# Hybrid encoder block: Q and K split where they are projected, both maps' scores of one half of the keys in one block, attention begun between the projection's last groups

## The reference, cut to what matters

```python
hn = rmsnorm(h, norm1_g[l])                     # h is (1, 2048, 1024), float32
proj = hn @ w_in[l]                             # (1, 2048, 2048): q, k, v, u, 512 columns each
q = proj[..., :512].reshape(bsz, s, 4, 2, 64)   # 4 heads, 2 maps, 64 wide
k = proj[..., 512:1024].reshape(bsz, s, 4, 2, 64)
v = proj[..., 1024:1536].reshape(bsz, s, 4, 128)
...
sc = einsum('bqhcd,bkhcd->bhcqk', qi, k) * scale     # two score maps per head, blocks of 128 queries
p = softmax(sc - slope * |qpos - kpos|)
a = p[:, :, 0] - lam * p[:, :, 1]
o = einsum('bhqk,bkhe->bqhe', a, v)
```

## Time and profile before

| what | value |
|---|---|
| device time, median of 3 runs (lowest to highest) | 2686.13 us (2683.91 to 2692.33) |
| profiled execution, span from first to last instruction | 2681.7 us |
| PE busy / DVE / ACT / POOL, share of the span | 96% / 78% / 53% / 12% |
| mean granted clock of PE, share of full speed | 0.981 |
| projection (PE) | 10.1 to 397.3 us |
| attention (PE) | 407.0 to 1006.1 us |
| S5 part, then output projection and MLP | 1009 us to the end |

### The profile page before, as it was taken

One profiled execution on the slowest core, in us unless ns is written; L12 is line 12 of the kernel. 1 busy time (PEld: TensorE's weight loads), 2 busy tenths in 40 slices (PEclk: granted clock), 3 DMA queues, 4 the chain that ended last, 5 costly groups with the idle time before them and its releaser, 6 DMA issues.

```text
span 2681.7 us, 32621 instructions
## 1 busy us (share of the span) xinstructions
PE 2562.9 (96%) x12804; PEld 2155.2 (80%) x12804; DVE 2093.3 (78%) x2074; ACT 1416.5 (53%) x1737; POOL 327.2 (12%) x221
## 2 busy tenths in 40 slices
PE   7998998999999998988989999999999999999998
PEld 5887777999999986766867888888887888888886
DVE  5866638999999976776898877677888886678885
ACT  3276616878787772224444566543334665543334
POOL 6310001101010003320334000000014000000003
PEclk8999998999999999998999999999999999999999
DMA  5356643020204008977565554452234664452221
GB/s 182 111 181 224 221 135 79 25 69 23 72 23 109 24 11 227 267 232 271 186 220 219 220 222 173 173 219 95 94 111 160 247 219 173 173 204 94 94 79 63
DMA packets 162520, 397.17 MB, mean 148 GB/s; under 512 B 29376, under 2 KB 86976, under 8 KB 134592
## 3 DMA queue, kind: packets, MB, share of 16 engines
q1 hardware_dynamic: 145664, 319.06, 35.9%
q10 hardware_dynamic: 16704, 76.03, 7.2%
HBM read 270.79 MB, written 122.16 MB: 147 GB/s over the span
## 4 chain that ended last, share of the span: by engine, by line
PE 44%; DVE 3%; POOL 1%; DMA 1%; issue 1%; ACT 0%; DVEq 0%; SPq 0%; ACTq 0%; POOLq 0%
PE ml_bank L2447 15%; PE ml_bank L2449 15%; PE ml_bank L2448 15%; POOL kp_tabs L2056 1%; DMA kp_low<-hn_s 1%; DVE ml_res L2327 0%; DVE ml_hb L2361 0%; DVE ml_b_split L2258 0%; DVE ml_w_split L2269 0%; DVE ml_res L2347 0%; DVE ml_rinv L2353 0%; PE ml_bank L2455 0%; DMA ml_hb<-h_s 0%; DMA hn_s<-ml_hb 0%; DVE kp_low L2282 0%
## 5 line engine op out<-in xcount | busy, mean ns | idle before, releaser
L2447 PE MATMUL ml_bank<-ml_b_split,ml_w_split 128*128 128x512 f32 x2016 | 788.8, 391 | 10.1 <-issue 9.8
L2448 PE MATMUL ml_bank<-ml_b_split,ml_w_split 128*128 128x512 f32 x2016 | 785.8, 390 | 0.0
L2449 PE MATMUL ml_bank<-ml_b_split,ml_w_split 128*128 128x512 f32 x2016 | 785.7, 390 | 0.0
L2447 PEld LDWEIGHTS ml_bank<-ml_b_split,ml_w_split 128*128 128x128 f32 x2016 | 379.3, 188 | 93.9 <-issue 14.6
L2448 PEld LDWEIGHTS ml_bank<-ml_b_split,ml_w_split 128*128 128x128 f32 x2016 | 379.6, 188 | 79.7 <-issue 1.2
L2449 PEld LDWEIGHTS ml_bank<-ml_b_split,ml_w_split 128*128 128x128 f32 x2016 | 379.4, 188 | 79.2
L2056 POOL TENSOR_TENSOR kp_tabs<-kp_tabs,ml_square 128x512 f32<-128x512 f32 x55 | 144.2, 2622 | 1266.4 <-ACT ml_square L2160 1259.9
L942 ACT ACTIVATE at_e<-at_e,at_neg_top 128x2048 f32<-128x2048 f32 x128 | 256.5, 2004 | 43.8 <-DVE at_neg_top L1027 43.8
L1148 PEld LDWEIGHTS at_pv<-at_v,at_a_t 128*128 128x128 f32 x2048 | 258.3, 192 | 16.4
L2327 DVE TENSOR_TENSOR ml_res<-ml_bank,ml_res 128x2048 f32<-128x2048 f32 x75 | 171.5, 2287 | 118.8 <-PE ml_bank L2449 118.8
L2094 ACT ACTIVATE ml_b_split<-kp_u_t 128x2048 fp32r<-128x2048 f32 x54 | 103.5, 1917 | 298.1 <-PE ml_bank L2449 298.1
(11 more groups left out here) (225 smaller groups left out, 4097.9 us busy)
## 6 DMA issues: line engine op xcount, KB each, us to landing
act_s<-ml_res ACTq DMA_DIRECT2D x32, 1024.0 KB, 4.0
kp_wide<-in_w_stream SPq DMA_DIRECT2D x18, 1024.0 KB, 5.1
kp_bp<-in_w_stream SPq DMA_DIRECT2D x18, 1024.0 KB, 5.5
kp_tabs<-in_w_stream SPq DMA_DIRECT2D x18, 1024.0 KB, 5.9
ml_r<-in_w_stream SPq DMA_DIRECT2D x18, 1024.0 KB, 6.7
tab_s<-kp_tabs ACTq DMA_DIRECT2D x32, 512.0 KB, 2.7
kp_low<-hn_s SPq DMA_DIRECT2D x16, 1024.0 KB, 5.5
kp_u_t<-hn_s SPq DMA_DIRECT2D x16, 1024.0 KB, 4.9
```

The costliest lines, as they stand in the source:

```text
L2447: pe.matmul(out, w_hi[:, w], b_hi[:, b], start=fresh and kt == 0, stop=False, skip_group_check=True)
L2448: pe.matmul(out, w_hi[:, w], b_lo[:, b], start=False, stop=False, skip_group_check=True)
L2449: last = pe.matmul(out, w_lo[:, w], b_hi[:, b], start=False, stop=kt == 3, skip_group_check=True)
```

## The change

What it does, by part:

1. **Split where projected.** For each of the 32 Q and K groups ACT makes the high part from `qku_out` into `v_out` (`keep_high`) and DVE subtracts it in place (`keep_low`); both are stored, to `hi_s` and `lo_s`. The buffers `qku_out` are free for group n+2 when both stores have landed (`stored`).
2. **Loads of the attention.** `load_k` is 8 DMAs of 512 KB per head, straight into `k_hi` and `k_lo`; `load_q` is 4 DMAs of 32 KB straight into `q_hl`, which has 2 buffers; Q of step n+2 is issued when the scores of step n are done. The splitting on ACT, DVE and POOL is gone from the attention. `head.load` is issued at n = 51 instead of 48.
3. **Both maps in one block.** The 8 matmuls of both maps for one half of the keys come together, and a PSUM slot belongs to a map. `combine` is done in two halves.
4. **Attention begins earlier.** Identity, distances, bias and lambda are made during the projection's last groups; K, two Q tiles and V are loaded in them; PE computes the scores of steps 0 and 1 behind groups 60 to 63, DVE their bias and maxima. Projection and attention share one block of instructions, without a joint end between them. The attention's tiles lie over tiles of the projection that are no longer used.

The diff, cut to its core (indentation changes left out; `...` where lines are left out):

```diff
+    def all_used(self, eng):
+        eng.wait_ge(self.outer_ready, 2 * NQU)
+        eng.wait_ge(self.tab_step, 4 * NGR)
+        eng.wait_ge(self.cycles_ready, 2 * NGR)
...
+    def stored(eng, i):
+        first = min(i, SECOND) // 2
+        wait(eng, qku_stored[i % 2], 32 * first + 16 * (i // 2 - first))
...
             if n < SECOND:
-                sp.dma_start(qk_s[g, :, t], qku_out[:, i % 2]).then_inc(qku_stored[i % 2], 16)
+                sp.wait_ge(hi_ready, i + 1)
+                sp.dma_start(hi_s[g, :, t], v_out[:, i % 2]).then_inc(qku_stored[i % 2], 16)
+                sp.wait_ge(lo_ready, i + 1)
+                sp.dma_start(lo_s[g, :, t], qku_out[:, i % 2]).then_inc(qku_stored[i % 2], 16)
...
             if n == NG - 7:
+                sp.wait_ge(rinv_ready, NTB)
+                sp.wait_ge(stats_done, NTB)
+                attention.load_lambda(sp)
+                sp.wait_ge(x_hi_ready, KD * (max(BLOCK_X) + 1))
                 sp.wait_ge(x_lo_ready, KD * (max(BLOCK_X) + 1))
                 sp.wait_ge(squares_ready, NTB)
+                prep.all_used(sp)
                 sp.wait_ge(w_lo_ready, NPIECE)
                 for i in range(2):
-                    sp.wait_ge(qku_stored[i], 16 * SECOND // 2)
-                shared.load_k(sp, qk_s, 0)
-                for i in range(4):
-                    shared.load_q(sp, qk_s, i)
+                    sp.wait_ge(qku_stored[i], 32 * SECOND // 2)
+                attention.load_k(sp, 0)
+                sp.wait_ge(prep.outer_stored, 16 * 2 * NQU)
+                for tile in range(2):
+                    attention.load_q(sp, tile)
+            if n == NG - 3:
+                for i in range(2):
+                    sp.wait_ge(v_stored[i], 16 * NV * NTB // 2)
+                attention.load_v(sp, 0)
+        for i in range(2):
+            sp.wait_ge(qku_stored[i], (32 * SECOND + 16 * NV * NTB) // 2)
...
+        def keep_high(n):                                   # ACT, after the evacuation of group n
+            act.wait_ge(qku_evacuated, n + 1)
+            stored(act, n)
+            act.activation(v_out[:, n % 2].bitcast(F32R), qku_out[:, n % 2], ACT.Copy).then_inc(hi_ready, 1)
...
         for n in range(NGROUP - 1, NG):                     # ACT's loop
             if g == NGROUP - 1 and b + 1 < NBLOCK and fresh_x(b + 1):
                 split_x(b + 1)
             if g == 1 and 0 < b < NTB:
                 stats(b)
+                keep_high(n - 1)
+            if n < SECOND and not (b and g == 0):
+                keep_high(n)
...
+        def keep_low(n):                                    # DVE
+            dve.wait_ge(hi_ready, n + 1)
+            dve.tensor_tensor(qku_out[:, n % 2], qku_out[:, n % 2], v_out[:, n % 2], ALU.subtract).then_inc(lo_ready, 1)
...
             prepare(n)
+            if n < SECOND:
+                keep_low(n)
+            if n == NG - 6:
+                attention.biases(dve)
+                attention.lambda_exponents(dve)
+            if n == NG - 5:
+                attention.lambda_difference(dve)
+            if n == NG - 4:
+                attention.add_bias(dve, 0, 0, 0)
+                attention.add_bias(dve, 0, 0, 1)
+            if n == NG - 3:
+                attention.second_half(dve, 0)
+            if n == NG - 2:
+                attention.first_half(dve, 1)
+            if n == NG - 1:
+                attention.second_half(dve, 1)
+                attention.combine(dve, 0, 1)
...
             group(n)                                        # PE
+            if n == NG - 4:
+                for before in range(NG - 6, NG - 4):
+                    evacuated(pe, before)
+                pe.wait_ge(rms_ready, NTB)
+            if n >= NG - 4:
+                attention.scores(pe, (n - NG + 4) // 2, n % 2)
...
+    def load_q(self, sp, n):
+        h, s = n // self.NQ, n % self.NQ
+        self.wait(sp, self.scores_done, 4 * (n - 1))
+        for c in range(2):
+            rows = slice(c * DH, (c + 1) * DH)
+            other = slice((1 - c) * DH, (2 - c) * DH)
+            for dst, src in ((rows, self.hi_s), (other, self.lo_s)):
+                sp.dma_start(self.q_hl[dst, n % 2, c].bitcast(F32), src[h, rows, s * P:(s + 1) * P])\
+                    .then_inc(self.q_loaded[n % 2], 16)
+    def load_k(self, sp, h):
+        self.wait(sp, self.scores_done, 4 * self.NQ * (h - 1))
+        for c in range(2):
+            for twin in range(2):
+                sp.dma_start(self.k_hi[h % 2][twin * DH:(twin + 1) * DH, c].bitcast(F32),
+                             self.hi_s[h + H, c * DH:(c + 1) * DH]).then_inc(self.k_loaded, 16)
+                sp.dma_start(self.k_lo[h % 2][c][twin * DH:(twin + 1) * DH].bitcast(F32),
+                             self.lo_s[h + H, c * DH:(c + 1) * DH]).then_inc(self.k_loaded, 16)
...
+    def first_half(self, dve, n):
+        for c in range(2):
+            self.add_bias(dve, n, 0, c)
+        self.coefficient(dve, n - 1)
+        self.combine(dve, n - 1, 0)
+    def second_half(self, dve, n):
+        for c in range(2):
+            self.add_bias(dve, n, 1, c)
+            self.negate_top(dve, n, c)
+    def scores(self, pe, n, half):
+        h = n // self.NQ
+        if half == 0:
+            pe.wait_ge(self.q_loaded[n % 2], 64 * (n // 2 + 1))
+            if n % self.NQ == 0:
+                pe.wait_ge(self.k_loaded, 128 * (h + 1))
+        cols = [...]
+        for c in range(2):
+            self.wait(pe, self.biased, 4 * n + 2 * half + c - 1)
+            for bank, keys in enumerate(cols):
+                out = self.score[:, c, bank * TB:(bank + 1) * TB]
+                pe.matmul(out, self.q_hl[:, n % 2, c], self.k_hi[h % 2][:, c, keys], start=True, stop=False)
+                last = pe.matmul(out, self.q_hl[:, n % 2, c], self.k_lo[h % 2][c][:, keys], start=False, stop=True)
+            last.then_inc(self.scores_done, 1)
...
+def phase_attention(block, a, head):
+    def _(sp):
+        for n in range(NS):
+            h, s = n // NQ, n % NQ
+            if n + 2 < NS:
+                a.load_q(sp, n + 2)
+            if s == 3 and h + 1 < H:
+                a.load_k(sp, h + 1)
+            if s == 6 and h + 1 < H:
+                a.load_v(sp, h + 1)
+            if n == NS - NQ + 3:
+                sp.wait_ge(a.pv_done, NS - NQ)
+                head.load(sp)
...
+    def _(act):
+        for n in range(NS + 3):
+            a.copy_turned(act, n - 2, (0, 1))
+            a.exponential(act, n - 1, 1)
+            a.copy_turned(act, n - 2, (2, 3))
+            a.copy_result(act, n - 3)
+            a.exponential(act, n, 0)
...
+    def _(dve):
+        for n in range(2, NS):
+            ...
+            a.first_half(dve, n)
+            a.second_half(dve, n)
+            a.combine(dve, n - 1, 1)
...
+    def _(pe):
+        pe.wait_ge(a.consts_step, 2)
+        for j in range(2):
+            a.turn(pe, 0, j)
+        for n in range(2, NS):
+            a.scores(pe, n, 0)
+            for j in range(2, 4):
+                a.turn(pe, n - 2, j)
+            for j in range(2):
+                a.values(pe, n - 2, j)
+            a.scores(pe, n, 1)
+            for j in range(2, 4):
+                a.values(pe, n - 2, j)
+            for j in range(2):
+                a.turn(pe, n - 1, j)
```

More of the change, by code:

```diff
@@ new lines, in phase_project @@
+    square_at = nc.sbuf_base
+    square = m.sb("square", [P, TB])
+    square_sum = m.sb("square_sum", [P, TB])
+    rms_b = m.sb("rms_b", [P, TB])
+    rinv_b = shared.bp[:].rearrange("p (n t) -> p n t", n=NTB)
+    rms_t = m.sb("rms_t", [P, NV])
+    rinv_t = m.sb("rinv_t", [P, NTB, NV])
+    gain = m.sb("gain", [P, KD])
+    ones = m.sb("ones", [P, P])
+    eps_c = m.sb("eps_c", [P, 1])
+    qku_out = m.sb("qku_out", [P, 2, TB])
+    v_out = m.sb("v_out", [P, 2, ATT])
+    banks = m.ps("banks", [P, BANKS + 2, TB])
@@ L779, in phase_attention @@
+    return block, attention
+class Attention:
     NQ = S // P
@@ L1176, in _ @@
             for j in range(4):
-                values(NS - 1, j)
+                a.values(pe, n, j)
+            if n + 1 < NS:
+                for j in range(2):
+                    a.turn(pe, n + 1, j)
 class SsmHead:
```

1230 lines of the change are left out of this document (555 added, 675 removed).

## The result

The change made the kernel slower: 2762.41 us median of 4 runs (2759.5 to 2763.18) against 2689.23 us for the kernel before beside it (2683.91 to 2693.99), ratio 1.0281, 95% interval 1.0263 to 1.0300. The forecast was 2719, its range 2685 to 2742: the sign was right, the size was not. The spans of the two profiled executions are 2681.7 and 2761.0 us.

| stretch | before | after | forecast | measured |
|---|---|---|---|---|
| up to the evacuation of group 60 | 381.2 | 423.2 | +21 | +42.0 |
| from there to step 3 | 56.5 | 53.3 | -5.6 | -3.1 |
| 60 steps | 544.5 | 580.7 | +29.5 - 9.7 | +36.2 |
| step 63 to the last matmul | 23.9 | 21.0 | -2.5 | -3.0 |
| S5 part, output projection, MLP | 1675.6 | 1682.8 | 0 | +7.2 |

What follows compares the result with a forecast made beforehand. PE was taken to set the attention's pace, 9.08 us a step. Terms +21 + 14.7 + 14.8 - 9.7 - 5.6 - 2.5 = +32.7 took span 2681.7 to 2714.4; plus 4.4 for the median, 2719; range 2685 to 2742.

Steps and rivals of the forecast that it cites:

- Part 1: Projection: splitting Q and K there adds waits for x_lo and low clock, +21 us, bounds +9 and +27.
- Blocks 1 and 2: Projection: DVE's split of x comes late, so PE waits 6.6 and 8.0 us for x_lo.
- block 5's wait: Projection: PE's wait for x_lo, 9.48 us before, grows by 3 as ACT falls behind; bounds 0 and 6.
- Part 2: Attention loads: Q queues behind doubled K and behind head.load, costing 14.7 and 14.8 us, 29.5 together.
- the three K waits: Attention, at three heads: PE waits 3.6 us for Q behind K, plus some 1.3 by the clock, each.
- Part 3: Attention's steady steps: two score blocks instead of four save 0.16 us a step, giving 8.86, 9.7 us over 60 steps.
- Part 4: Attention's start: the earlier begin gains 5.6 us by step 3.
- the two waits: Attention's start: PE waits 7.2 us behind group 60 and about 6 before step 2.
- The tail: Attention's end: combine in halves lets turns begin earlier, 21.4 us instead of 23.9, 2.5 gained.
- Q was held: Attention loads, opposite of a rival: Q not held by K, without the 29.5 us, 2689; chance 0.12.
- the projection did not absorb the split: Projection, opposite of a rival: split absorbed, +21 becomes about +1, 2699; chance 0.12.
- DVE did not become the attention's bound: Attention, opposite of a rival: DVE bounds it, step 9.16 us or more, 2732; chance 0.07.

Runs made afterwards that it cites:

- e2: Changed kernel without keep_high and keep_low, unsplit Q and K stored twice: 2726.8 us.
- e3: Changed kernel with keep_high moved behind ACT's own w split and tables of the same group in groups 25 to 31: 2747.4 us.
- e14: Changed kernel with both split instructions of groups 24 to 31 on POOL instead of ACT and DVE: 2747.0 us.
- e16: Changed kernel with each S5 outer product's three instructions spread over three neighbouring groups: 2750.9 us.
- e9: Changed kernel with, in groups 24 to 31, high part on DVE, keep_low and last four w loads earlier; S5 outer products moved to groups 33 to 53: 2751.2 us.
- e12: Changed kernel with only the S5 outer products moved, from groups 26 to 53 to groups 33 to 53: 2760.0 us.
- e13: Changed kernel with e9's edits but other outer-product groups, plus four Q buffers, earlier start loads and x split earlier in every block: 2697.3 us.
- e17: Changed kernel with e15's edits, e16's edit and K of head 0 loaded by halves of the keys: 2674.2 us, ratio to the kernel before 0.9959.
- e1: Changed kernel with each head's K loaded in two parts, V at tile 7 and the S5 part's first loads in three parts: 2724.0 us.
- e6: Changed kernel with four Q buffers instead of two and Q issued two steps earlier, K and S5 loads still in bursts: 2718.6 us.
- e15: Changed kernel with four Q buffers, earlier start loads, x split earlier for blocks 1 and 2, w loads one store earlier and e14's edit: 2694.7 us.
- e5: Changed kernel with the attention's first loads issued behind group 56's store instead of 57's, step 2's Q behind 62's instead of 63's: 2749.2 us.

## Why the prediction was right or wrong

- **Part 1** failed, and with it the number. Blocks 1 and 2 were right in place and near in size (6.6 and 8.0 forecast, 5.77 and 6.17 measured). The step that failed is "0.6 more puts it behind by some 3 us, and block 5's wait, which hangs on ACT's table stores, grows by 3 (bounds 0 and 6)": it grew by 22.2. The lower clock took 6.0 where 3.6 was forecast, and block 3, forecast at nothing, waited 1.89. I had added up ACT's work, 0.6 us a group, and not what waits for what. `keep_high` makes ACT wait for DVE's evacuation in each group, DVE waits for ACT's w_hi and SP for both. e2 shows that the split's two instructions are the cause. e3 (order alone), e14 (coupling off both engines) and e16 (shorter pieces) each take 9 to 16 us from block 5 with no less work in all. In e9, e12 and e13 moving the long pieces moved the wait. No single edit that keeps the split brought block 5 back to 9.48 us (e12 came nearest, with 12.48); e17, with several, did (8.91), and with no wait of 1 us at blocks 6 and 7.
- **Part 2** was right as a mechanism: e1 and e6 remove the waits by two different cures. Forecast 29.5, measured 36.2: the three K waits were 5.3 instead of 3.6, `head.load` 10.0 instead of 12.9, and the clock cost 2.5 each, not 1.3 and 1.9.
- **Q behind K.** Q waited in all four cases, as the earlier trace rows had it. Of the Trainium skill, DMA: Bandwidth & Descriptors, section Queues, rings and completion order, the prediction used one half. The other half says that the write which raises a semaphore lands only after every earlier write of the same DMA engine, across its queues; that agrees with Q here, and with e15, where the V stores of SP's queue were late behind K on ACT's.
- **Part 3** was wrong: -9.7 forecast, about 0 measured (9.08 us a step on average either way, an undisturbed one 0.05 us longer after). The forecast step of 8.86 us is an undisturbed 9.02 less 0.16; the 9.08 that the prediction gives as the pace is the average. Single gaps are 0.32 and 0.23, as it read them, but the narrow matmuls were left out. The Trainium skill, TensorE: Matmul & The Clock Gate (Back-to-back issue gap), gives the gap by a formula with the number of columns and nothing on what ran before. By that the regrouping is worth nothing; the sums here agree within 0.05 us a step, the single gaps do not.
- **Part 4**: -5.6 forecast and -3.1 measured; the two waits were 9.56 and 5.58 instead of 7.2 and some 6. The tail gave 3.0, forecast 2.5.
- **The part nobody touched**, from the S5 part's first transposes to the end, is 7.2 us longer in the profile after, where the forecast had 0. In other profiled executions of this study it is 1672.2 (e2), 1673.1 (e5), 1674.4 (e1), 1680.6 (e6) and 1682.8 (e17), against 1671.8 before and 1679.0 after. What sets it in this range stays open, and single profiled executions can't say whether the change has a part in it.
- **The rivals.** None came: Q was held, the projection did not absorb the split, DVE did not become the attention's bound. The case that did come, a bound of Part 1 far too low, had no chance of its own. The range was made from bounds on durations; block 5's term, whose mechanism I had not walked through, had 0 and 6.
